# Unread products of the identity at PE's waits in a streaming encoder step

## The chip, the cores and the metric

The kernel runs on 1 core of one Trainium2 chip. TensorE (PE) multiplies, VectorE (DVE) and ScalarE (ACT) work element by element, GpSimd (POOL) helps, SyncE (SP) issues loads. Loading the weights of a product into PE's array is listed apart as PEld. The metric is the device time of one execution in microseconds, lower is better.

## What is computed

One inference step of two layers, for 512 prompt frames and 32 sample frames in one pass (T = 544 columns). Everything is f32. Cut to what matters here:

```python
def ffn_half(x, g_pre, g_post, w_gu, w_dn):
    return x + 0.5 * rmsnorm(swiglu(rmsnorm(x, g_pre), w_gu, w_dn), g_post)

def trunk_layer(l, x, ...):
    x = ffn_half(x, g[0], g[1], w_ffn_gu[l, 0], w_ffn_dn[l, 0])
    u = rmsnorm(x, g[2])
    qa, ka, va, qb, kb, vb = jnp.split(u @ w_in[l], 6, axis=-1)
    ...   # oa: band attention, 8 heads x 64; ob: differential attention, 4 heads x 128
    ob = rmsnorm(ob, subln_g[l]) * (1.0 - lam_init)
    mix = jnp.concatenate([oa, ob], axis=-1) @ w_out[l]
    x = x + rmsnorm(mix, g[3])
    oc = cross_attend(rmsnorm(x, g[4]) @ w_cq[l], mem_k, mem_v) @ w_co[l]
    x = x + rmsnorm(oc, g[5])
    return ffn_half(x, g[6], g[7], w_ffn_gu[l, 1], w_ffn_dn[l, 1])
```

Outputs are the two streams' results and the keys and values of every layer.

## The kernel before

Activations lie transposed: 8 blocks of 128 model columns on the partitions, 544 frames on the free axis, in two halves of 272 (half 0, half 1). A matrix product splits both sides into a high and a low part (`u_hi`, `u_lo`; `w_hi`, `w_lo`) and sums three products, `w_hi`·`u_hi`, `w_hi`·`u_lo`, `w_lo`·`u_hi`. This is `product` (line 607): three matmuls of 128x272 for each block and half. A **chunk** is all 8 blocks of one output tile, 24 matmuls for each half. SP loads the weights in chunks, ACT cuts `w_hi`, DVE takes the difference `w_lo`; both rings have two slots, and a slot is cut anew once PE has counted `chunk_done`.

Each engine runs its own list in the order in which it is written, and engines meet at semaphores. Nothing is planned while it runs.

**A hand-over** is the place where one stage ends and the next begins with a normalised input. The new `x` needs the norm of the last stage's output `y`: PE sums the squares over the partitions (`norm_y`, line 622), ACT takes the root, DVE the inverse, PE spreads it over the partitions (`spread_y`, lines 582 and 629: two turns and a small product of the identity), DVE multiplies `y` by it and adds it to `x`, ACT cuts `u_hi`, DVE `u_lo`. Half 0 is ahead of half 1. PE meanwhile runs `first_chunks`, in this order: first chunk of half 0, whose block k waits for `u_lo` of that block, with `norm_y` of half 1 before block 4 (`before`); `spread_y` of half 1 (`between`); second chunk of half 0; then both chunks of half 1, the first again block by block behind `u_lo`. `late_norms` calls it with `before` and `between` in five hand-overs: at the start of three feed-forward stages (all but the very first) and of the two combined input projections. The hand-over into cross-attention calls `first_chunks` without them. The pre-norm of the new stage is not applied to `u`; its sums of squares (`norm_x`) and its spread (`spread_x`) follow a little later, and the product's result is scaled by `r_pre`.

**Attention** follows a table of steps (`attention`, `OWN` for the two own head groups). Scores take two slots of PSUM in turn. At its end the outputs of the four differential heads, tiles 4 to 7, are turned (`"use": "out"`): the turn of tile 4 waits for `head_normed`, that is for the norm of all four heads, taken after the last value product; ACT takes the root, DVE scales `o_nat` head by head, and then DVE cuts `u_hi` and `u_lo` of every tile from the slot. `w_out` follows.

`ident` is an f32 identity of 128x128. The PSUM banks 0 and 1 take the two halves of the first chunk.

Of the kernel before, what the change touches and what calls it, by code (L numbers as in the profile page):

```python
# [72 lines left out]
def rows_of(i):  # L73
    return 128 if i < NT else SAMPLE
# [96 lines left out]
def build(nc, x_prompt, x_sample, mem_prompt, cache_a_k, cache_a_v, cache_b_k, cache_b_v,  # L171
# [8 lines left out]
    def place(name, shape, dtype=F32, offset=None):  # L180
        size = int(np.prod(shape[1:])) * 4
        if offset is None:
            offset = at[0]
            at[0] += (size + 31) // 32 * 32
        return nc.alloc_sbuf_tensor_at(name, shape, dtype, offset=offset)
# [17 lines left out]
    ident = place("ident", [128, 128])  # L203
# [82 lines left out]
    psum = nc.alloc_psum_tensor("psum", [128, 8, 512], F32)  # L286
# [61 lines left out]
    def slot_ap(slot, rows, n, start=0):  # L348
        return flat[0:rows, slot * 1024 + start:slot * 1024 + start + n]
# [32 lines left out]
    def settled(engine):  # L382


        engine.sem_inc(passed)
# [193 lines left out]
    def _(pe):  # L579
        def turn(out, src):  # L580
            rows = src.shape[0]
            return pe.transpose(out, src, ident[0:rows, 0:rows])  # L582
# [15 lines left out]
        def product(slot, b, bank, xs, start, stop, half=None):  # L598
            hi, lo = xs
            wh = w_hi[:, slot, b * 128:(b + 1) * 128]  # L600
            wl = w_lo[:, slot, b * 128:(b + 1) * 128]
            n = hi.shape[-1]
            halves = [(0, H), (H, T)] if n == T else [(0, n)]
            for w, xx, s0, s1 in ((wh, hi, start, False), (wh, lo, False, False), (wl, hi, False, stop)):
                for part, (c0, c1) in enumerate(halves):
                    if half in (None, part):
                        pe_last[0] = pe.matmul(psum[:, bank + part, 0:c1 - c0], w, xx[:, c0:c1], start=s0, stop=s1)  # L607

        def half_chunk(pair, slot, bank, inputs, blocks, half, first, last, before=None):

            pe.wait_ge(w_lo_ready, 2 * pair + slot + 1)
            for b, k in enumerate(blocks):
                if before:
                    before(k)
                product(slot, b, bank, inputs(k), first and b == 0, last and b == len(blocks) - 1, half)
            return pe_last[0]

        def token_sums(sums, half, bank, col):

            for i, start in enumerate(GROUPS):  # L620
                t = half * H + start
                mm = pe.matmul(psum[:, bank, col + i:col + i + 1], sums[:, t:t + 128], ones[:, 0:1], start=True, stop=True)  # L622
            return mm
# [31 lines left out]
        def first_chunks(pair, q, before=None, between=None):  # L655

            def arrived(half):
                def wait(k):
                    pe.wait_ge(u_lo_ready, 16 * q + 8 * half + k + 1)
                    if before and half == 0 and k == 4:  # L660
                        before()
                return wait
            half_chunk(pair, 0, 0, u_in, range(KD), 0, True, True, arrived(0))
            if between:
                between()
            half_chunk(pair, 1, 2, u_in, range(KD), 0, True, True)
            half_chunk(pair, 0, 0, u_in, range(KD), 1, True, True, arrived(1)).then_inc(chunk_done, 1)
            half_chunk(pair, 1, 2, u_in, range(KD), 1, True, True).then_inc(chunk_done, 1)

# [71 lines left out]
        def attention(l, steps):  # L741
            for step in steps:
                for it in step["uses"]:
                    slot = it["slot"] % 2
                    if it["slot"] >= 2:
                        pe.wait_ge(*slot_free(it["slot"] - 2, l))
                    if it["use"] == "cache":
                        tile, width = it["tile"], 128
                        if it["of_kind"] == "C":
                            pe.wait_ge(cmk_loaded, l * 16 + 16)  # L750
                            src = cmk_nat[:, tile, :]
                        else:
                            pe.wait_ge(kc_loaded[tile % 2], l * 64 + 32 * (it["of_kind"] == "B") + 16 * (tile // 2 + 1))
                            src = kc_nat[:, tile % 2, :]
                        for m in range(4):
                            mm = turn(slot_ap(slot, 128, 128, m * 128), src[:, m * 128:(m + 1) * 128])
                    elif it["use"] == "out":
                        if it["tile"] >= 4:
                            pe.wait_ge(head_normed, l * 8 + 2 * (it["tile"] - 3))
                        elif it["slot"] < OWN_COUNT["slot"]:  # L760
                            pe.wait_ge(o_kept, l * TOTAL["unit"] + 2 * (NT + 1) * (it["tile"] + 1))
                        else:
                            pe.wait_ge(o_kept, l * TOTAL["unit"] + OWN_COUNT["unit"] + (NT + 1) * (it["tile"] + 1))
                        for i in range(NT + 1):
                            mm = turn(slot_ap(slot, 128, rows_of(i), i * 128),
                                      o_nat[0:rows_of(i), it["tile"] % 4, i, :])
                    else:
                        mm = score(l, it, slot)
                    mm.then_inc(slot_ready, 1)
                for u in step["turn"]:  # L770
                    ub, rows = u["unit"] % 2, rows_of(u["i"])
                    if u["kind"] == "B":
                        pe.wait_ge(combined, l * TOTAL["combined"] + u["combined"] + 1)
                    else:
                        pe.wait_ge(expd, l * TOTAL["expd"] + u["scores"][0]["expd"] + 1)
                    if u["unit"] == 0:
                        pe.wait_ge(nat_kept, l * 32 + 32)
                    if u["unit"] >= 2:
                        pe.wait_ge(turned_kept, l * TOTAL["turned"] + UNITS[u["unit"] - 2]["turned"])
                    settled(pe)  # L780
                    p = probs_at(u["scores"][0])
                    n = keys_of(u)
                    for k in range((n + 127) // 128):
                        keys = min(128, n - k * 128)
                        mm = turn(psum[0:keys, 4 + ub, k * rows:(k + 1) * rows], p[0:rows, k * 128:k * 128 + keys])
                    mm.then_inc(turned, 1)
                for u in step["value"]:
                    ub, rows, h = u["unit"] % 2, rows_of(u["i"]), u["h"]
                    pe.wait_ge(turned_kept, l * TOTAL["turned"] + u["turned"])
                    if u["unit"] >= 2:  # L790
                        pe.wait_ge(o_kept, l * TOTAL["unit"] + u["unit"] - 1)
                    n = keys_of(u)
                    if u["i"] == NT:
                        if u["kind"] == "C":
                            pe.wait_ge(cmv_loaded, l * 16 + 16)
                        else:
                            pe.wait_ge(vc_loaded, l * 32 + (16 if u["kind"] == "A" else 32))

                    tiles = (n + 127) // 128
                    tile = h // 2 if u["kind"] == "A" else h  # L800
                    for k in range(tiles):
                        keys = min(128, n - k * 128)
                        at_ = tile * 128 + (512 if u["kind"] == "B" else 0)
                        if u["kind"] == "C":
                            v = (mv_nat if u["i"] < NT else cmv)[:, k, h * 128:(h + 1) * 128]
                        elif u["i"] == NT and k < 4:
                            v = vc[:, k, tile * 128:(tile + 1) * 128]
                        else:
                            v = v_nat[0:keys, k, at_:at_ + 128]
                        mm = pe.matmul(psum[0:rows, 6 + ub, 0:128],  # L810
                                       probs_t[0:keys, ub, k * rows:(k + 1) * rows], v,
                                       start=k == 0, stop=k == tiles - 1)
                    mm.then_inc(values_done, 1)
# [38 lines left out]
        for l in range(DEPTH):  # L852
# [65 lines left out]
            for m in range(KD + 1):  # L918
                if m < KD:
                    if m >= 2:  # L920
                        pe.wait_ge(kv_kept, l * 8 + m - 1)
                    chunk(base + AT_CKV + m // 2, m % 2, m % 2, lambda k: (m_hi[:, k, :], m_lo[:, k, :]), range(KD),
                          True, True, count=memory_norms if m == 0 else None).then_inc(chunk_done, 1)
# [802 lines left out]
```

## Time and profile before

| | us |
|---|---|
| median of 3 runs | 2788.9 |
| lowest, highest | 2785.92, 2790.43 |
| profiled execution, device time | 2787.24 |
| its span in the trace | 2785.4 |
| PE busy | 2610.1 (94%) |
| DVE busy | 1272.3 (46%) |
| ACT busy | 900.8 (32%) |
| mean granted clock of PE | 0.968 |

The span is the trace's own time, some 2 us less than the device time. Times in the trace count from the span's start; places are named by them. "[2.48 <-DVE w_lo L1285]" behind a row says that the engine sat idle for 2.48 us and which instruction released it. The end of a PE row is modelled, so distances between products are read from start to start. The granted clock is given as a share of 2.4 GHz: 1.00 is the full rate, 0.50 is 1.2 GHz, and a value between them is a stretch with both. "x2" behind a row means two records merged.

### The profile page before, as it was taken

The numbers are of one execution on the slowest core, as the hardware profiler recorded it, in microseconds if no ns is written. First come the engines' busy times: TensorE is split into PE (matmuls) and PEld (weight loads), VectorE is DVE, ScalarE is ACT, GpSimd is POOL, SyncE is SP. The second block draws the span as 40 slices with busy tenths as digits, with TensorE's granted clock in tenths as the row PEclk, the third lists the DMA queues.
The fourth block names the chain that finished last, engine by engine and source line by source line (L and its number), as shares of the span: only waits on it lengthen the run. The fifth ranks groups of instructions, "written<-read, shape, count | busy, mean of one in ns | idle before, by whom it ended". The sixth has DMA issues, their size and how long they took to land.

```text
span 2785.4 us, 48225 instructions
## 1 busy us (share of the span) xinstructions
PE 2610.1 (94%) x19513; PEld 2471.8 (89%) x19513; DVE 1272.3 (46%) x2307; ACT 900.8 (32%) x1576; POOL 67.9 (2%) x199
## 2 busy tenths in 40 slices
PE   7999998999898889999989999989898988999998
PEld 6999998986587789999989999989755977999998
DVE  4444325345846554442254442253457555444323
ACT  3222223224533432222232222232344534322221
POOL 1000000001100000000000000000111000000000
PEclk9999999999989999999999999999998998999999
DMA  5233332330023023233223233233310321223321
GB/s 178 85 88 90 91 91 86 116 120 25 24 91 105 18 68 90 84 95 94 67 69 88 85 92 93 73 101 116 105 40 31 92 75 31 83 83 90 97 84 64
DMA packets 383972, 229.81 MB, mean 83 GB/s; under 512 B 6636, under 2 KB 371198, under 8 KB 383840
## 3 DMA queue, kind: packets, MB, share of 16 engines
q1 hardware_dynamic: 378272, 206.59, 25.3%
q0 software_dynamic: 4368, 16.92, 1.7%
q10 hardware_dynamic: 1200, 4.46, 0.4%
q8 instruction: 93, 1.52, 0.2%
q14 instruction: 39, 0.32, 0.0%
HBM read 214.39 MB, written 18.79 MB: 84 GB/s over the span
## 4 chain that ended last, share of the span: by engine, by line
PE 83%; DVE 11%; ACT 2%; issue 2%; DMA 1%; DVEq 0%; SPq 0%; ACTq 0%
PE psum L607 73%; PE psum L810 3%; PE psum L582 3%; PE psum L829 2%; DVE u_lo L1280 2%; DVE w_lo L1285 2%; DVE x L1326 1%; DVE probs L1469 1%; PE psum L622 1%; DVE y_ffn L1320 1%; DVE y_mix L1320 1%; ACT w_hi L993 1%; PE psum L823 1%; PE psum L831 0%; DMA w_raw<-in_w_ffn_gu 0%
## 5 line engine op out<-in xcount | busy, mean ns | idle before, releaser
L607 PE MATMUL psum<-u_hi,w_hi 128*128 128x272 f32 x4096 | 906.8, 295 | 62.1 <-DVE w_lo L1285 24.2
L607 PE MATMUL psum<-u_hi,w_lo 128*128 128x272 f32 x4096 | 894.3, 292 | 0.0
L607 PE MATMUL psum<-u_lo,w_hi 128*128 128x272 f32 x4096 | 892.3, 292 | 0.0
L607 PEld LDWEIGHTS psum<-u_hi,w_hi 128*128 128x128 f32 x4096 | 671.7, 193 | 72.8 <-DVE u_lo L1280 28.3
L993 ACT ACTIVATE w_hi<-w_raw 128x1024 fp32r<-128x1024 f32 (+1 forms) x336 | 376.8, 1121 | 1105.6 <-PE psum L607 1091.2
L607 PEld LDWEIGHTS psum<-u_lo,w_hi 128*128 128x128 f32 x4096 | 672.5, 193 | 0.0
L607 PEld LDWEIGHTS psum<-u_hi,w_lo 128*128 128x128 f32 x4096 | 667.9, 193 | 0.0
L1285 DVE TENSOR_TENSOR w_lo<-w_raw,w_hi 128x1024 fp32r<-128x1024 f32 (+1 forms) x336 | 436.5, 1299 | 348.3 <-ACT w_hi L993 348.3
L607 PE MATMUL psum<-h_hi,w_hi 128*128 128x272 f32 x1408 | 305.7, 288 | 0.5
L607 PE MATMUL psum<-h_lo,w_hi 128*128 128x272 f32 x1408 | 304.5, 287 | 0.0
L607 PE MATMUL psum<-h_hi,w_lo 128*128 128x272 f32 x1408 | 304.4, 287 | 0.0
L607 PEld LDWEIGHTS psum<-h_hi,w_hi 128*128 128x128 f32 x1408 | 226.0, 189 | 1.3 <-DVE w_lo L1285 1.3
L607 PEld LDWEIGHTS psum<-h_lo,w_hi 128*128 128x128 f32 x1408 | 226.3, 188 | 0.0
L607 PEld LDWEIGHTS psum<-h_hi,w_lo 128*128 128x128 f32 x1408 | 226.2, 188 | 0.0
L1372 DVE TENSOR_TENSOR up<-psum,r_pre 128x544 f32<-128x544 f32 x88 | 63.7, 724 | 292.1 <-PE psum L607 292.1
L1368 DVE TENSOR_TENSOR gate<-psum,r_pre 128x544 f32<-128x544 f32 x88 | 63.8, 725 | 248.1 <-PE psum L607 232.7
L1013 ACT ACTIVATE square<-psum 128x544 f32<-128x544 f32 (+1 forms) x76 | 42.0, 552 | 333.8 <-PE psum L607 333.8
L1137 ACT ACTIVATE probs<-probs,negmax 128x256 f32<-128x256 f32 (+4 forms) x136 | 81.1, 596 | 140.8 <-DVE negmax L1469 140.6
L1297 DVE TENSOR_TENSOR sumsq<-sumsq,square 128x544 f32<-128x544 f32 (+1 forms) x60 | 36.7, 611 | 179.3 <-ACT square L1013 178.7
L1594 DVE TENSOR_TENSOR fresh<-psum,r_pre 128x544 f32<-128x544 f32 x48 | 34.6, 724 | 153.0 <-PE psum L607 146.6
L829 PE MATMUL psum<-qk,q_pad 128*128 128x384 f32 (+3 forms) x256 | 94.8, 471 | 3.2 <-DVE negmax L1469 2.2
L810 PE MATMUL psum<-v_nat,probs_t 128*128 128x128 f32 (+1 forms) x528 | 85.8, 290 | 10.2 <-ACT probs_t L993 8.9
(189 smaller groups left out, 2097.1 us busy)
## 6 DMA issues: line engine op xcount, KB each, us to landing
w_raw<-in_w_ffn_gu SPq DMA_DIRECT2D x176, 512.0 KB, 3.8
w_raw<-in_w_ffn_dn SPq DMA_DIRECT2D x64, 704.0 KB, 4.6
w_raw<-in_w_in SPq DMA_DIRECT2D x48, 512.0 KB, 3.7
w_raw<-in_w_out SPq DMA_DIRECT2D x16, 512.0 KB, 3.9
w_raw<-in_w_ckv SPq DMA_DIRECT2D x16, 512.0 KB, 3.8
bias_tab_dram<-bias_rev_dram POOLq DMA_DIRECT2D x1, 5120.0 KB, 21.3
table<-bias_tab_dram SPq DMA_DIRECT2D x16, 320.0 KB, 2.9
out<-k_nat POOLq DMA_DIRECT2D x4, 1024.0 KB, 5.0
```

The costliest lines, as they stand in the source:

```text
L582: return pe.transpose(out, src, ident[0:rows, 0:rows])
L607: pe_last[0] = pe.matmul(psum[:, bank + part, 0:c1 - c0], w, xx[:, c0:c1], start=s0, stop=s1)
L810: mm = pe.matmul(psum[0:rows, 6 + ub, 0:128], probs_t[0:keys, ub, k * rows:(k + 1) * rows], v, start=k == 0, stop=k == tiles - 1)
L829: return pe.matmul(slot_ap(slot, rows, keys_of(u)), q, k[:, 0:keys_of(u)], start=True, stop=True)
L993: return act.activation(out, src, ACT.Copy, scale=scale)
L1013: act.activation(sq, src, ACT.Square).then_inc(y_squared, 1)
L1137: act.activation(p, p, ACT.Exp, bias=negmax[0:rows, s % 8:s % 8 + 1], scale=-1.0, accum_out=rowsum[0:rows, s % 8:s % 8 + 1]).then_inc(expd, 1)
L1280: return dve.scalar_tensor_tensor(out=out, in0=a, scalar=scalar, in1=b, op0=op0, op1=op1)
L1285: dve.tensor_tensor(w_blocks(w_lo, slot, n), w_blocks(w_raw, slot, n), w_blocks(w_hi, slot, n).bitcast(F32), ALU.subtract).then_inc(w_lo_r ...
L1320: dve.tensor_tensor(part, part, r, ALU.mult).then_inc(y_normed, 1)
L1368: dve.tensor_tensor(two(gate[:, parity, :]), banks(4 * parity), two(r_pre[:, :]), ALU.mult).then_inc(gate_scaled, 1)
L1372: dve.tensor_tensor(two(up[:, parity, :]), banks(4 * parity + 2), two(r_pre[:, :]), ALU.mult).then_inc(up_scaled, 1)
```

## The change

`spin(n, out)` issues n products of the identity with itself, 128x128 in f32, each with start and stop set. Their result is overwritten by the next real product at the same place, and no instruction reads it. They are placed in three places:

- in `first_chunks`, if it was given `before`: 6 ahead of the first chunk of half 0, into bank 0
- also there: 20 between the second chunk of half 0 and the first of half 1, into bank 1
- in `attention`, 10 ahead of the wait for `head_normed` of tile 4, into the slot that this turn writes

That makes 5 x 26 products in the hand-overs and 2 x 10 in attention, 150 in all. No other engine's list changes, and PE's list is the old one with these rows put in.

```diff
--- before.py
+++ after.py
@@ -615,6 +615,11 @@
                 product(slot, b, bank, inputs(k), first and b == 0, last and b == len(blocks) - 1, half)
             return pe_last[0]
 
+        def spin(n, out):
+
+            for _ in range(n):
+                pe.matmul(out, ident[:, :], ident[:, :], start=True, stop=True)
+
         def token_sums(sums, half, bank, col):
 
             for i, start in enumerate(GROUPS):
@@ -660,10 +665,14 @@
                     if before and half == 0 and k == 4:
                         before()
                 return wait
+            if before:
+                spin(6, psum[:, 0, 0:128])
             half_chunk(pair, 0, 0, u_in, range(KD), 0, True, True, arrived(0))
             if between:
                 between()
             half_chunk(pair, 1, 2, u_in, range(KD), 0, True, True)
+            if before:
+                spin(20, psum[:, 1, 0:128])
             half_chunk(pair, 0, 0, u_in, range(KD), 1, True, True, arrived(1)).then_inc(chunk_done, 1)
             half_chunk(pair, 1, 2, u_in, range(KD), 1, True, True).then_inc(chunk_done, 1)
 
@@ -755,6 +764,8 @@
                         for m in range(4):
                             mm = turn(slot_ap(slot, 128, 128, m * 128), src[:, m * 128:(m + 1) * 128])
                     elif it["use"] == "out":
+                        if it["tile"] == 4:
+                            spin(10, slot_ap(slot, 128, 128))
                         if it["tile"] >= 4:
                             pe.wait_ge(head_normed, l * 8 + 2 * (it["tile"] - 3))
                         elif it["slot"] < OWN_COUNT["slot"]:
```

The places in PE's list, in the first hand-over between a feed-forward stage and the input projection. Before, where the first chunk of half 0 follows the down projection (`h_hi`, `h_lo` are its inputs):

```order
L607 MATMUL psum<-h_hi,w_hi 128x272
L607 MATMUL psum<-h_lo,w_hi 128x272
L607 MATMUL psum<-h_hi,w_lo 128x272
L607 MATMUL psum<-u_hi,w_hi 128x272 [waits u_lo_ready,w_lo_ready]
L607 MATMUL psum<-u_lo,w_hi 128x272
L607 MATMUL psum<-u_hi,w_lo 128x272
```

and the same place now:

```order
L607 MATMUL psum<-h_hi,w_hi 128x272
L607 MATMUL psum<-h_lo,w_hi 128x272
L607 MATMUL psum<-h_hi,w_lo 128x272
L621 MATMUL psum<-ident 128x128 x6
L607 MATMUL psum<-u_hi,w_hi 128x272 [waits u_lo_ready,w_lo_ready]
L607 MATMUL psum<-u_lo,w_hi 128x272
```

The six products stand ahead of the instruction that waits for `w_lo` and `u_lo`, and wait for nothing themselves. Between the halves, now:

```order
L607 MATMUL psum<-u_hi,w_hi 128x272
L607 MATMUL psum<-u_lo,w_hi 128x272
L607 MATMUL psum<-u_hi,w_lo 128x272
L621 MATMUL psum<-ident 128x128 x20
L607 MATMUL psum<-u_hi,w_hi 128x272 [waits u_lo_ready,w_lo_ready]
L607 MATMUL psum<-u_lo,w_hi 128x272
L607 MATMUL psum<-u_hi,w_lo 128x272
```

The twenty follow the last product of the second chunk of half 0, and the first block of half 1 is queued behind them. At the end of attention, where tile 4 is turned, before:

```order
L810 MATMUL psum<-vc,probs_t 32x128 x3
L810 MATMUL psum<-v_nat,probs_t 32x128
L582 MATMUL psum<-ident,o_nat 128x128 [waits head_normed,biased]
L582 MATMUL psum<-ident,o_nat 128x128 x3
L582 MATMUL psum<-ident,o_nat 128x32
```

and now:

```order
L821 MATMUL psum<-vc,probs_t 32x128 x3
L821 MATMUL psum<-v_nat,probs_t 32x128
L621 MATMUL psum<-ident 128x128 [waits biased]
L621 MATMUL psum<-ident 128x128 x9
L582 MATMUL psum<-ident,o_nat 128x128 [waits head_normed]
```

The wait for the slot (`biased`) moved to the first of the ten; the wait for the norm stays with the turn.

## Rows read from the trace of the kernel before

**Rows 1.** The page's chain that ended last, by engine: shares of the span

```profile
PE 83%; DVE 11%; ACT 2%; issue 2%; DMA 1%; DVEq 0%; SPq 0%; ACTq 0%
```

**Rows 2.** PE's waits, whole span: waiting line, releaser, us in total, times, longest

```profile
PE psum L607 <- DVE u_lo L1280: 24.1, 21, 2.1
```

**Rows 3.** Timeline, PE, 439 to 463: start, us, operation, count, [idle before, releaser]

```profile
439.09 0.39 PE L607 MATMUL psum<-u_hi,w_hi 128*128 128x272 f32 x1 [2.48 <-DVE w_lo L1285]
...
442.58 1.44 PE L622 MATMUL psum<-ones,sumsq 128*128 128x1 f32 x6 [0.67 <-DVE u_lo L1280]
...
446.99 0.60 PE L607 MATMUL psum<-u_hi,w_hi 128*128 128x272 f32 x1 [1.40 <-DVE u_lo L1280]
...
449.23 0.57 PE L607 MATMUL psum<-u_hi,w_hi 128*128 128x272 f32 x1
449.60 0.43 PE L607 MATMUL psum<-u_lo,w_hi 128*128 128x272 f32 x1
449.83 0.43 PE L607 MATMUL psum<-u_hi,w_lo 128*128 128x272 f32 x1
...
458.55 0.40 PE L607 MATMUL psum<-u_hi,w_hi 128*128 128x272 f32 x1 [1.15 <-DVE u_lo L1280]
...
462.54 0.52 PE L607 MATMUL psum<-u_hi,w_hi 128*128 128x272 f32 x2
```

**Rows 4.** Chain in order of time: a dense stretch, start, us, records

```profile
490.91 6.02 PE psum L607 x48
```

**Rows 5.** Windows, PE: window, length, busy (records), granted clock, DMA share, GB/s

```profile
440.00:452.00 12.00, 9.92 (x43) 0.50 0.50 143
452.00:454.00 2.00, 2.00 (x14) 0.73 1.00 378
984.00:986.00 2.00, 2.00 (x12) 0.61 0.42 128
1817.00:1819.00 2.00, 1.18 (x9) 0.86 0.00 0
1833.00:1835.00 2.00, 2.00 (x10) 0.50 0.00 0
```

**Rows 6.** Timeline, PE, hand-over at 973: second chunk, first product after half 1

```profile
984.16 0.57 PE L607 MATMUL psum<-u_hi,w_hi 128*128 128x272 f32 x1
...
997.47 0.52 PE L607 MATMUL psum<-u_hi,w_hi 128*128 128x272 f32 x2
```

**Rows 7.** Value products in attention: two groups of the timeline, the page's group

```profile
636.63 1.16 PE L810 MATMUL psum<-v_nat,probs_t 128*128 128x128 f32 x8
...
638.48 1.06 PE L810 MATMUL psum<-vc,probs_t 128*32 128x128 f32 x8
...
L810 PE MATMUL psum<-v_nat,probs_t 128*128 128x128 f32 (+1 forms) x528 | 85.8, 290 | 10.2 <-ACT probs_t L993 8.9
```

**Rows 8.** Timeline at the turn of the heads' outputs: DVE, then PE

```profile
770.22 0.77 DVE L1438 TENSOR_SCALAR u_hi<-psum,sub_gain 128x544 fp32r<-128x544 f32 x1
...
768.04 2.61 PE L582 MATMUL psum<-ident,o_nat 128*128 128x128 f32 x10 [2.60 <-DVE o_nat L1611]
...
776.42 0.82 PE L607 MATMUL psum<-u_hi,w_hi 128*128 128x272 f32 x2 [1.70 <-DVE u_lo L1280]
```

**Rows 9.** Timeline, PE, hand-over at 1813

```profile
1813.00 0.39 PE L607 MATMUL psum<-u_hi,w_hi 128*128 128x272 f32 x1 [2.48 <-DVE w_lo L1285]
...
1816.49 0.83 PE L622 MATMUL psum<-ones,sumsq 128*128 128x1 f32 x6 [1.39 <-DVE u_lo L1280]
...
1820.29 0.59 PE L607 MATMUL psum<-u_hi,w_hi 128*128 128x272 f32 x1 [2.11 <-DVE u_lo L1280]
...
1822.52 0.57 PE L607 MATMUL psum<-u_hi,w_hi 128*128 128x272 f32 x1
...
1831.85 0.42 PE L607 MATMUL psum<-u_hi,w_hi 128*128 128x272 f32 x1 [1.16 <-DVE u_lo L1280]
...
1837.24 0.42 PE L607 MATMUL psum<-u_hi,w_hi 128*128 128x272 f32 x2
```


## The prediction

> **What bounds the kernel now.** I read the chain of waits first, then PE's waits, then PE's own rows with the granted clock beside them. The chain ends on PE for 83% of the span and on DVE for 11% [rows 1]. The change adds only work for PE, so it can save time in one way alone, by keeping PE's clock up, and only where PE is last. PE's waits show where: 24.1 us for `u_lo` in 21 waits, beside those for `w_lo` and for the heads' `o_nat` [rows 2, 3, 8]. A large part of them lies in the five hand-overs that carry the new products (at about 439, 973, 1394, 1813 and 2346 us) and before the two attention outputs (768 and 2140 us).
>
> One hand-over, at 439 us [rows 3]. PE waits 2.48 us for `w_lo`, runs four blocks of half 0, waits until 442.58 for block 4 and the sums, and until 446.99 for blocks 6 and 7. Then come the spread of `inv_y`, from 449.23 the second chunk of half 0 (24 products), and the two chunks of half 1 (48 products), paced by `u_lo` until 458.55. At 462.54 PE goes on with full products. Products stand 0.227 us apart here (449.60 to 449.83) against 0.125 us in dense stretches (48 in 6.02 us) [rows 3, 4]. The granted clock says why: 0.50 from 440 to 452, the lower level of 1.2 GHz, back at 2.4 GHz within 452 to 454 [rows 5].
>
> The cold clock costs less than it seems. It delays the end only where PE is the last to arrive: in the sums, in blocks 6 and 7 and in the spread, because DVE waits for the spread. After that DVE paces half 1, and the cold second chunk fits into waits. From the first product of the second chunk to the first after half 1 PE takes 13.31 us at 449 (462.54 - 449.23), with 17 cold products, and the same 13.31 us at 984 (997.47 - 984.16), with some 6 cold ones [rows 3, 6]: the clock's return, late or early, made no difference.
>
> **What one filler costs.** A product of two f32 operands is two records of PE: the three sums stand as x6. The nearest rows are the value products of attention: two groups of 8 records last 1.16 and 1.06 us, and one record 0.29 us on the mean, which leaves 7 steps of 0.124 and 0.110 us [rows 7]. For a run of 12 to 40 alike I take 0.115. Bounds: 0.105 below, since a product of 272 columns needs 0.125 and these have 128 columns in a wider type, 0.125 above. So 6 products are 1.4 us, 20 are 4.6 us (4.2 to 5.0), 10 are 2.3 us. At the low clock f32 records stand some 0.24 us apart (10 in 2.61 us) [rows 8], which would make it 2.9, 9.7 and 4.8 us.
>
> On a page: the Trainium skill ("TensorE: Matmul & The Clock Gate", section "Back-to-back issue gap") gives about 81 ns for each matmul of 128 columns in a stream with weight loads. By it the 20 products would be an estimated 3.2 us and my total would fall by 7 us, to about -2. The trace's f32 rows read 0.110 to 0.124, so the sum goes by them.
>
> **Part 1, six products before half 0.** 1.4 us in a wait of 2.48 us: nothing to pay, PE is back 1 us before `w_lo`. If that cover were gone it would be 1.4 us each. They should keep the clock up until the first blocks. What that is worth one hand-over of before already shows, the one at 1813, where the clock stayed up through the blocks and sums and fell only within 1817 to 1819 [rows 5]. There blocks 6 and 7 started 3.80 us after the sums (1816.49 to 1820.29) instead of 4.41 us (442.58 to 446.99) [rows 3, 9]. So 0.6 us in each of the other four. But in the same hand-over the clock then fell in the two waits around the sums (1.39 and 2.11 us idle), and the blocks at 1820.29, the spread and the start of the second chunk ran cold. The six fillers put nothing into those waits. So I expect each changed hand-over to look like 1813 up to the spread, and that one to stay as it is.
>
> **Part 2, twenty products between half 0 and half 1.** They stand after the second chunk of half 0. PE's work from that chunk's first product to the end of half 1 becomes 72 products at 0.125 us = 9.0, restarts 0.2, fillers 4.6: 13.8 us at the full clock, against 13.31 us now, where DVE sets the pace. So the fillers do not fit: they exceed the waits that are there, even warm. To that comes what of the second chunk is cold, 0.10 us a product: 0.6 us (6 products) to 1.7 us (17), and 0.3 us more where it starts 0.6 us earlier, on average 1.2 us. Before, this was hidden; now PE is the last. 15.0 us, so +1.7 us, less 0.6 us from part 1: +1.1 us, in four hand-overs +4.4 us. At 1813 the stretch takes 14.72 us now (1822.52 to 1837.24), since the clock fell a second time while PE waited for `u_lo`: 0.50 in 1833 to 1835 [rows 5, 9]. The fillers remove that fall; 15.0 - 14.72 = +0.3 us, and another 0.3 us since ACT cuts the next weights and squares x only when the first chunk of half 1 is done. Who waits behind: ACT's `w_hi`, the squares and DVE's `sumx` (for which PE waits near 465), then the next chunks; nothing after half 1 in a feed-forward hand-over has slack, as PE runs densely to the spread of `inv_x`. So delays go to the end one to one.
>
> **Part 3, ten products before the turn of tile 4.** 2.3 us in a wait of 2.60 us [rows 8]: hidden at the full clock. The ten turns after it would be warm, but DVE does not wait for them: it runs without idle time before `u_hi` at 770.22, and PE starts the output projection on `u_lo` at 776.42. Between lie ten more turns and waits, the last of 1.70 us, so the projection should start cold as now. I take 0. Bounds: +2 us each if the ten ran cold (4.8 us in 2.6), -1.9 us each if the clock held through to the projection (18 products 0.10 us faster).
>
> **Sum.** 4.4 + 0.6 + 0 = +5.0 us. Made against the profiled execution, 2787.24 us, that is 2792.2; the median of before is 1.7 us above that execution, and I put the same difference on it: 2788.9 + 5.0 = 2793.9 us.
>
> **The rivals.**
> A, the clock is held (faster). If the fillers keep 2.4 GHz through the waits at the sums too, the spread comes some 1.5 us earlier (0.6 sums, 0.6 blocks 6 and 7, 0.3 spread), against +0.5 us for 13.8 in place of 13.31: -1.0 us in four, and at 1813 -0.9 - 0.9 = -1.8. Sum -6, time about 2783; with a warm output projection -10. For it: the fillers give PE work just ahead, and the clock did stay up over a wait of 2.48 us before 1813 [rows 9]. Against it: 1813 itself. It decides by the clock at blocks 6 and 7. The Trainium skill (same page, section "HAM oscillation — how this bites in real kernels") blames the fall on waits between bursts that are longer than those that remain here, and recommends dense work; by that rule the clock would hold and this rival's time would come. The trace speaks against it: the clock fell at 1818 with idle times of 1.39 and 2.11 us.
> B, the clock returns late (slower). If the sums stay cold and the clock comes back as late as at 439 in every hand-over, the surcharge is 1.7 to 2.0 us and nothing is won first: 15.7 - 13.3 = +2.4 in four and +1 at 1813, sum +11, time about 2800. For it: the row at 440 to 452. Against it: at 984 it was back within 984 to 986 [rows 5]. It decides where over 10 products of the second chunk run cold.
> C, it comes out even, between -3 and +2 us: fillers at 0.105 us or below (-2 us), the clock back at once in most places (-4 us), or the fillers without any effect on the clock and mostly in waits. Time about 2788.
>
> **How the numbers follow.** Forecast 0.57, A 0.16, B 0.12, C 0.15. A measurement of this kernel tells some 0.2% (5.6 us) from no change. The forecast's own range is +2 to +8 us, so 0.23 of its 0.57 lie beyond +5.6. Slower: 0.23 + B 0.12 = 0.35. Faster: most of A, 0.14. Same: 0.34 + 0.02 + 0.15 = 0.51. The range leaves out the outer part of A and of B: 2784 to 2801.
>
> **What would show it.** Right: f32 records of `ident` 0.11 to 0.125 us apart; clock 1.0 at the first blocks and sums, 0.50 at blocks 6 and 7; no wait for `u_lo` left in half 1; the stretch from the second chunk's start to the first product after half 1 at 14.4 to 15.6 us against 13.31; half-1 products dense and warm; 776.42 unchanged against its own attention. Wrong: clock 1.0 at the spread (A), waits for `u_lo` still there after the twenty (cheaper fillers), or a late turn of tile 4.

## The result, and the profile after

The change makes the kernel slightly slower: the median of 20 runs is 2792.9 us against 2788.3 us for 20 runs of the kernel before. The ratio is 1.0018, 95% interval 1.0011 to 1.0026, that is +4.6 us where +5.0 us had been forecast (the interval is +3 to +7 us). One point of caution first: the profiled execution of after took 2786.4 us, the lowest of its 20 runs, with a span of 2784.6 us, 0.8 us less than before's. So the profile does not show the loss as a whole; it shows what the hand-overs cost, and something else that went better in this one execution.

The page's chain, after (before: [rows 1], PE 83% and DVE 11%):

```profile
PE 85%; DVE 10%; ACT 2%; issue 2%; DMA 1%; DVEq 0%; SPq 0%; ACTq 0%
```

PE's wait for `u_lo` in the waits of after (us in all, number, longest; before 24.1 us in 21 waits [rows 2]):

```profile
PE psum L607 <- DVE u_lo L1291: 12.8, 8, 2.2
```

The waits halved, PE took a larger share of the chain, and the time did not fall: a wait was filled, and a little more than filled. The first hand-over shows where. The timeline of PE of after (start, us, operation; before [rows 3]):

```profile
435.94 1.50 PE L621 MATMUL psum<-ident 128*128 128x128 f32 x12
438.57 0.40 PE L607 MATMUL psum<-u_hi,w_hi 128*128 128x272 f32 x1 [1.13 <-DVE w_lo L1296]
...
442.06 0.83 PE L627 MATMUL psum<-ones,sumsq 128*128 128x1 f32 x6 [1.38 <-DVE u_lo L1291]
...
445.86 0.59 PE L607 MATMUL psum<-u_hi,w_hi 128*128 128x272 f32 x1 [1.49 <-DVE u_lo L1291]
...
448.09 0.57 PE L607 MATMUL psum<-u_hi,w_hi 128*128 128x272 f32 x1
...
451.90 4.62 PE L621 MATMUL psum<-ident 128*128 128x128 f32 x40
...
462.37 0.41 PE L607 MATMUL psum<-u_hi,w_hi 128*128 128x272 f32 x2
```

The same hand-over's granted clock (window, length, PE busy, clock, DMA share, GB/s), and in the last line that of the second hand-over, whose first block starts at 971 here and at 973 in before:

```profile
438.00:442.00 4.00, 2.08 (x12) 1.00 0.47 131
443.00:449.00 6.00, 4.51 (x20) 0.50 0.39 119
451.00:456.00 5.00, 5.00 (x46) 1.00 0.80 297
456.00:462.00 6.00, 6.00 (x51) 1.00 0.00 1
976.00:985.00 9.00, 7.60 (x34) 0.50 0.20 58
```

Read from top to bottom: the six fillers end 1.1 us before `w_lo` is there; the clock is at 2.4 GHz over the first blocks (before it was at 1.2 GHz from 440 on [rows 5]); it falls at the sums, between a wait of 1.38 us and one of 1.49 us, so the blocks behind the sums, among them 6 and 7, the spread and the start of the second chunk run at 1.2 GHz (products 0.227 us apart); the twenty take 4.6 us at the full clock; and after them PE has no wait left up to the first full product. That stretch, from the second chunk's first product to the first after half 1, is 14.28 us (462.37 - 448.09), where before had 13.31 us.

Read in the same way, the five hand-overs of both profiles (us, from start to start). The last column goes on to the sums of `x` (`ones,sumx`), the next thing for which PE may have to wait:

| hand-over at | sums to blocks 6, 7: before, after | second chunk to end of half 1: before, after | first block to end: before, after | first block to sums of `x`: before, after |
|---|---|---|---|---|
| 439 | 4.41, 3.80 | 13.31, 14.28 | 23.45, 23.80 | 26.47, 26.92 |
| 973 | 4.41, 4.27 | 13.31, 15.33 | 23.99, 25.86 | 30.12, 31.86 |
| 1394 | 4.41, 3.86 | 13.30, 14.21 | 23.43, 23.79 | 29.55, 29.79 |
| 1813 | 3.80, 3.94 | 14.72, 14.09 | 24.24, 23.76 | 26.49, 26.88 |
| 2346 | 4.41, 4.33 | 13.31, 15.28 | 23.99, 25.87 | 30.12, 31.87 |
| sum | | | 119.10, 123.08 | 142.75, 147.32 |

Up to the end of half 1 the hand-overs cost 4.0 us more. At 1813 this mark comes too early, as PE's timeline shows, first in before (the hand-overs at 439 and at 1813):

```profile
465.56 1.50 PE L622 MATMUL psum<-ones,sumx 128*128 128x1 f32 x12 [0.51 <-DVE sumx L1344]
...
1839.49 1.39 PE L622 MATMUL psum<-ones,sumx 128*128 128x1 f32 x12
```

and in after:

```profile
465.49 1.60 PE L627 MATMUL psum<-ones,sumx 128*128 128x1 f32 x12 [0.71 <-DVE sumx L1355]
...
1837.86 1.50 PE L627 MATMUL psum<-ones,sumx 128*128 128x1 f32 x12 [0.71 <-DVE sumx L1355]
```

At 1813 before reached the end of half 1 late and then had no wait for `sumx`; after reached it earlier and waited 0.71 us. So the 0.5 us that after seems to win there is a loss of 0.4 us one step later. Up to the sums of `x` the five hand-overs cost 4.6 us more. How much of that is the change and how much this pair of executions is less sure: the kernel with the ten alone and the one with the held projection, both described below, have the hand-overs of before, and took 144.8 and 144.9 us to the same mark.

The rest of the profiled execution was 5.4 us shorter than before's (2784.6 - 147.32 against 2785.4 - 142.75). No work was changed there but the ten products in attention. The clock was low for less of it: in windows of 2 us, PE was busy at 1.2 GHz outside the hand-overs for an estimated 100 us in before and 90 us in after. One such place, in attention, as PE's window in before:

```profile
699.00:705.00 6.00, 5.71 (x22) 0.50 0.00 0
```

and the same window in after:

```profile
699.00:705.00 6.00, 5.09 (x36) 1.00 0.11 40
```

The places where the clock falls are not the same ones in each execution. The 20 runs of before spread over 10 us and those of after over 14 us, and in after the mean granted clock goes with the time: 0.974 in the shortest run, 0.970 in the longest.

The last place, at the turn of the heads' outputs, PE's timeline in after (before: [rows 8]):

```profile
766.14 4.58 PE L621 MATMUL psum<-ident 128*128 128x128 f32 x20
770.55 1.54 PE L582 MATMUL psum<-ident,o_nat 128*128 128x128 f32 x10
...
777.56 0.82 PE L607 MATMUL psum<-u_hi,w_hi 128*128 128x272 f32 x2 [2.19 <-DVE u_lo L1291]
```

and DVE's there:

```profile
771.37 0.79 DVE L1449 TENSOR_SCALAR u_hi<-psum,sub_gain 128x544 fp32r<-128x544 f32 x1 [0.32 <-PE psum L582]
```

In this execution attention ended at the low clock, and the ten took 4.58 us where the prediction had 2.3. They ended after the turn could have begun, and DVE, which had not waited before, waited 0.32 us.

### The profile page after: what moved, and what is told of

Same layout as the page of the kernel before. It is cut to its first block, busy times and chain, and to the rows that moved or that the text cites. A ratio compares the mean times of both kernels' runs of the same rounds, so it can differ in the third digit from the quotient of the medians.

```text
span 2784.6 us, 48823 instructions
## 1 busy us (share of the span) xinstructions
PE 2630.0 (94%) x19813; PEld 2495.4 (90%) x19813; DVE 1272.6 (46%) x2307; ACT 898.9 (32%) x1576; POOL 67.6 (2%) x199
## 4 chain that ended last, share of the span: by engine, by line
PE 85%; DVE 10%; ACT 2%; issue 2%; DMA 1%; DVEq 0%; SPq 0%; ACTq 0%
PE psum L607 73%; PE psum L821 3%; PE psum L582 3%; PE psum L840 2%; DVE w_lo L1296 2%; PE psum L621 1%; DVE u_lo L1291 1%; DVE probs L1480 1%; DVE x L1337 1%; PE psum L627 1%; ACT w_hi L1004 1%; PE psum L834 1%; DVE y_mix L1331 1%; PE psum L842 0%; DVE y_ffn L1331 0%
```

## The experiments

Each difference is against the kernel of the change; each ratio against the kernel before, from interleaved runs. A line `pass` stands where products are left out. None leaves out or changes any part of the computation: the products in question are read by nobody. The kernel with forty, the first one with filled waits and the two with all of it together have only 5 or 6 runs each, the others 11 or 12.

**The six alone.**

```diff
-                spin(20, psum[:, 1, 0:128])
+                pass
-                            spin(10, slot_ap(slot, 128, 128))
+                            pass
```

> Only the six products ahead of half 0 are left of the change. My theory (they fit into the wait for w_lo, and keep the clock at 2.4 GHz over the first blocks and the sums): blocks 6 and 7 of half 0 start 3.8 us after the sums instead of 4.4 us, in four of five hand-overs, of which some is lost again where the clock comes back later: -1 to -2 us against before. If the six themselves were the loss (they delay the first block), +1.4 us in each of five hand-overs, +7 us. If they have no effect on the clock, 0.

Measured: 2785.7 against 2788.0 us, ratio 0.9991 (0.9980 to 1.0003), so -2.4 us with an interval that just includes no change. The sums to blocks 6 and 7 took 3.88, 4.33, 3.80, 3.80 and 3.80 us. The time from the first block to the end of half 1 was 118.4 us over the five, 0.7 us less than before's 119.1; in two of them the clock fell again in the waits of half 1, as it had at 1813 before (14.67 and 14.49 us for the stretch). Up to the sums of `x` it was 142.0 us against 142.75. The six are not the loss; that they gain anything lies within the noise of the medians.

**The twenty alone.**

```diff
-                spin(6, psum[:, 0, 0:128])
+                pass
-                            spin(10, slot_ap(slot, 128, 128))
+                            pass
```

> Only the twenty products between half 0 and half 1 are left. My theory (they exceed the waits of half 1 by 0.5 us with a warm second chunk, and every cold product of that chunk is now paid for): more than the whole change, since the sums stay cold: +6 to +8 us against before, and no wait for u_lo left in half 1. If the loss of the change lies in the six or in attention, 0 or less here; if the twenty hold the clock and that pays, below 0.

Measured: 2792.1 against 2788.0 us, ratio 1.0022 (1.0012 to 1.0031). By the ratio that is +6 us, the lower end of what was expected; by the two medians it is +4.0 us, below it. No wait for `u_lo` in half 1; first block to end summed 124.2 us, +5.1 us, and to the sums of `x` 148.4 us, +5.7 us. The loss sits here. That the six give back a part of it is what the profiles show (148.4 us here, 147.3 us in the change); the times of the two kernels (1.0022 and 1.0018) are too close to tell.

**The ten in attention alone.**

```diff
-                spin(6, psum[:, 0, 0:128])
+                pass
-                spin(20, psum[:, 1, 0:128])
+                pass
```

> Only the ten products ahead of the turn of tile 4 are left. My theory (hidden in the wait for head_normed, and DVE paces what follows): 0, between -1 and +1 us; the output projection starts cold as before. If they hold the clock through to the projection: -3.8 us. If they run at the low clock or past the wait: +2 to +4 us.

Measured: 2787.8 against 2788.0 us, ratio 1.0001 (0.9992 to 1.0010): nothing. In both layers of this profile they ran at the full clock, 2.50 us, and the time from the last value product to the projection was 11.38 us, that of before to the last digit. In the profiles where the last value products ran at the low clock it was 11.6 us without the ten (the kernel with the twenty alone, both layers) and 11.9 to 12.0 us with them, as in the change. In the kernel with forty, where the clock came back during the ten (3.03 us), it was 11.6 us. So they are free or cost 0.3 to 0.4 us, by the clock that they find. In this profile one hand-over, which has no products of the change, had a second fall of the clock: 15.56 us from the second chunk to the end of half 1 at 1394, 13.3 us in the other four.

**Forty in place of twenty.**

```diff
-                spin(20, psum[:, 1, 0:128])
+                spin(40, psum[:, 1, 0:128])
```

> The whole change, with 40 products in place of 20 between the halves. My theory says that PE is the last to arrive already with 20, so that all of the added time is paid: 20 products of 0.23 us (two records of 0.115 us) in five hand-overs, +23 us against the change, +28 us against before (1.010). If waits were left behind the twenty, less: with 1 us of wait left in each hand-over +23 us against before, with 2 us +18 us.

Measured: 2815.6 us, ratio 1.0094 (1.0079 to 1.0108). By the ratios that is +26 us against before and +21 us against the change (1.0018), by the medians +28 and +23 us. PE's timeline in its first hand-over:

```profile
449.37 0.57 PE L607 MATMUL psum<-u_hi,w_hi 128*128 128x272 f32 x1
...
453.14 9.09 PE L621 MATMUL psum<-ident 128*128 128x128 f32 x80
...
468.09 0.41 PE L607 MATMUL psum<-u_hi,w_hi 128*128 128x272 f32 x2
```

The stretch is 18.72 us, 4.44 us more than the change's 14.28, and the fillers are 4.47 us longer. Everything that is added between the halves is paid at once: with the twenty PE was already the last.

**Ten in place of twenty.**

```diff
-                spin(20, psum[:, 1, 0:128])
+                spin(10, psum[:, 1, 0:128])
```

> The whole change with 10 products in place of 20 between the halves (2.3 us instead of 4.6). My theory: PE's work over second chunk and half 1 is then 11.5 us warm and about 12.7 with some cold products, below DVE's pace of 13.31, so waits for u_lo come back in half 1, the fillers cost nothing, the gain of the six (some 0.5 us each) stays and no second fall of the clock is left: -2 to -5 us against before (0.9985), that is -7 to -9 us against the change. If the twenty cost time for another reason than their length (a start of the stream, memory traffic), only half of the loss goes: +2 us against before.

Measured: 2784.3 against 2786.9 us, ratio 0.9991 (0.9983 to 1.0000), -2.6 us. PE's timeline in its fourth hand-over:

```profile
1819.92 0.57 PE L607 MATMUL psum<-u_hi,w_hi 128*128 128x272 f32 x1
...
1824.09 2.39 PE L621 MATMUL psum<-ident 128*128 128x128 f32 x20
...
1829.24 0.39 PE L607 MATMUL psum<-u_hi,w_hi 128*128 128x272 f32 x1 [0.49 <-DVE u_lo L1291]
...
1833.23 0.52 PE L607 MATMUL psum<-u_hi,w_hi 128*128 128x272 f32 x2
```

The stretch is 13.31 us, in all five between 13.29 and 13.32, although blocks 6 and 7 and the start of the second chunk still ran cold: DVE's pace is back as the bound, and there was no second fall. First block to end sums to 116.5 us, -2.6 us against before, and to the sums of `x` 141.0 us, -1.8 us; that the first is just the medians' difference is chance. Half the fillers turn the loss into a gain about as large as its own uncertainty.

**Filling the waits in which the clock fell** (rival A of the prediction, made true by more products).

```diff
+                    if before and half == 0 and k in (4, 6):
+                        spin(6 if k == 4 else 7, psum[:, 1, 0:128])
-                spin(20, psum[:, 1, 0:128])
+                spin(10, psum[:, 1, 0:128])
```

> As the kernel with 10 between the halves, and with 6 products more behind block 3 of half 0 (ahead of the sums) and 7 more behind block 5, in the two waits in which the clock fell in the change. It tests the rival that the clock can be held through a hand-over. If so, sums, blocks 6 and 7, the spread and the second chunk all run at 2.4 GHz, the spread comes 1.5 us earlier than before and DVE's pace follows: -1.5 us in four hand-overs, more where before had a second fall, -7 to -9 us against before (0.997). If the clock falls in spite of it, the fillers run at 0.24 us a record and delay the sums: +5 us or more.

Measured: 2777.4 us, ratio 0.9963 (0.9951 to 0.9976), -9.5 us. Its first hand-over, PE's timeline:

```profile
441.75 1.50 PE L621 MATMUL psum<-ident 128*128 128x128 f32 x12
...
444.83 1.72 PE L621 MATMUL psum<-ident 128*128 128x128 f32 x14
...
447.10 0.39 PE L607 MATMUL psum<-u_hi,w_hi 128*128 128x272 f32 x1 [0.55 <-DVE u_lo L1293]
...
448.36 0.37 PE L607 MATMUL psum<-u_hi,w_hi 128*128 128x272 f32 x1
...
461.66 0.52 PE L607 MATMUL psum<-u_hi,w_hi 128*128 128x272 f32 x2
```

and the window of PE over all of it (busy, clock, DMA share, GB/s):

```profile
438.00:462.00 24.00, 20.97 (x161) 1.00 0.42 138
```

The clock stays at 2.4 GHz. From blocks 6 and 7 to the second chunk it takes 1.26 us (447.10 to 448.36) where before took 2.24 us [rows 3], and the sums cost 0.6 us less: the spread comes 1.6 us earlier, and DVE's pace of 13.3 us starts from there. First block to end sums to 110.3 us, -8.8 us, and to the sums of `x` 134.75 us, -8.0 us.

**The same with twenty again, and with none between the halves.** The first keeps `spin(20, ...)`, the second has

```diff
-                spin(20, psum[:, 1, 0:128])
+                pass
```

beside the two added lines of the filled kernel.

> The filled hand-overs with 20 products between the halves again instead of 10: the price of the twenty where no product is cold. Prediction's term: 72 products at 0.125, restarts 0.2 and fillers 4.6 are 13.8 us against DVE's pace of 13.31, so +0.5 us a hand-over, +2.5 us against the kernel with ten (0.9963): about 0.9972 of before, -8 us. If the twenty cost their full difference of 2.3 us a hand-over in spite of the waits, +11.5 us, 1.0004 of before; if PE were not the last, 0.9963 as with ten.

> The filled hand-overs without any product between the halves. If the ten there do nothing once the clock is held over the sums, 0.9963 as with them. My theory: without them PE idles three times while it waits for u_lo in half 1 (0.3 to 0.6, 1.1 and 1.2 us or more, since it arrives earlier than before), the clock falls there in some hand-overs and the end of half 1 runs cold: +2 to +6 us against the kernel with ten, 0.9970 to 0.9985 of before.

With twenty: 2776.7 against 2787.0 us, ratio 0.9965 (0.9953 to 0.9976). That is not to be told from ten (0.9963), so the medians neither show nor exclude the expected 2.5 us; they exclude 11.5. The profile has the number itself, on PE's timeline:

```profile
445.38 0.37 PE L607 MATMUL psum<-u_hi,w_hi 128*128 128x272 f32 x1
...
448.48 4.63 PE L621 MATMUL psum<-ident 128*128 128x128 f32 x40
...
458.95 0.42 PE L607 MATMUL psum<-u_hi,w_hi 128*128 128x272 f32 x2
```

13.57 us, the same within 0.01 in all five hand-overs, against 13.3 with ten: 0.3 us too long where no product is cold, 1.3 us in all. In the change the excess over 13.31 us was 6.6 us in the five hand-overs. So about four fifths of it is cold products, and the fillers' length only takes away the room for them.

With none: 2779.1 us, ratio 0.9971 (0.9960 to 0.9981), about 2 us more than with ten, at the low end of what was expected; the two intervals overlap. In its profile the stretch took 14.70, 13.29, 15.16, 15.16 and 14.46 us: in four of five the clock fell in the waits of half 1, and in one it did not. Its clock there:

```profile
1406.00:1412.00 6.00, 5.82 (x30) 0.61 0.02 5
```

So fillers between the halves are worth having in these profiles (13.3 us in all five hand-overs with ten); the medians alone do not prove it.

**Holding the clock up to the output projection.** No filler in the hand-overs; the ten ahead of tile 4 stay.

```diff
+                    if it["use"] == "out" and it["tile"] >= 6:
+                        spin(8 if it["tile"] == 6 else 3, psum[:, 6, 0:128])
...
+            spin(8, psum[:, 6, 0:128])
             pe.wait_ge(split_lo, l * TOTAL["split"] + OWN_COUNT["split"])
```

> Only at the end of attention: ten products ahead of the turn of tile 4, 8 ahead of tile 6, 3 ahead of tile 7, 8 ahead of the output projection, all in waits for DVE; no filler in the hand-overs. If the clock is held through to the projection, its first 18 products run at 0.125 us instead of 0.227: -1.9 us in each of two layers, -3.8 us against before (0.9986). If my reading of the waits is off and the fillers delay the turns that DVE waits for, +1 to +4 us. If the clock falls anyway, 0.

Measured: 2782.5 against 2786.9 us, ratio 0.9985 (0.9976 to 0.9994), -4.4 us. The clock, where before had 1.2 GHz until 780:

```profile
770.00:782.00 12.00, 12.00 (x96) 1.00 0.18 66
```

This was the other end of part 3's bounds, and the ten ahead of the first turn alone could not do it (the experiment with the ten alone). Its profile accounts for only half of the 4.4 us. The fillers make the projection start later after the last value product (12.33 and 12.19 us in the two layers, before 11.38), and the first turn of the memory behind the projection comes 1.0 and 1.15 us sooner (42.49 and 42.35 us after the last value product, before 43.50).

**All of it together, and two more places.** The filled hand-overs and the held projection in one kernel; then also 12 products ahead of the last turn of the memory values and 8 ahead of the first chunk of cross-attention's queries:

```diff
+                    if m == KD:
+                        spin(12, psum[:, 5, 384:512])
                     pe.wait_ge(kv_kept, l * 8 + t + 1)
...
+            spin(8, psum[:, 5, 384:512])
             pe.wait_ge(kv_nat, l * 8 + 8)
```

> The fillers of the filled hand-overs and those up to the output projection together. The parts lie in different places and each shifts all that follows, so they should add: -8 - 3.8, about -12 us against before (0.9957). If the gain of one is given back at the other's place, less than the larger of the two.

> All held, and in addition 12 products ahead of the last turn of the memory values (PE waits 3.27 us there) and 8 ahead of the first chunk of the cross-attention's queries (2.19 us), where the clock fell in the trace of the kernel with all held, with some 20 products at 0.227 us after it. If it is held, -2 us in each of two layers: about 0.9937 - 0.0014 = 0.9923 of before. If the twelve (2.8 us) run into the low clock, or past the wait, +1 to +3 us.

Measured: 2770.2 against 2786.9 us, ratio 0.9937 (0.9922 to 0.9952), then 2765.1 against 2787.0 us, ratio 0.9923 (0.9909 to 0.9937). The parts add at least: -9.5 and -4.4 make -13.9 us against -16.7 measured, within the intervals; the -12 us (0.9957) that had been expected was too little and lies outside the interval. The two further places bring the expected 0.14%, 4 us, though the intervals of the two kernels overlap. The clock in the second, over the end of the memory's projection, the hand-over to the queries and their chunks:

```profile
848.00:884.00 36.00, 33.70 (x275) 1.00 0.43 132
```

This version is faster than the kernel before by 22 us and than the change by some 27 us.

## Why the prediction was right, step by step

The mechanism is shown: the loss needs the twenty, it goes with half of them, and it grows with forty by the full time that they add. That the number came within 0.4 us is in part luck, since one execution of a kernel and the next differ by more, and since single terms missed in both directions.

- **PE at the hand-overs, DVE's pace behind it.** Right. DVE's 13.3 us from the second chunk to the end of half 1 stood in every kernel in which PE's own work fitted and the clock did not fall again: with none, with six and with ten fillers.
- **The price of a filler.** 0.115 us a record was taken, the trace has 4.62 us for 40 records and 1.50 us for 12, so 0.111 us for each one more (3.12 over 28). At the low clock 20 records took 4.41 us up to the next row (766.14 to 770.55), 0.22 us each where 0.24 had been taken. The Trainium skill ("TensorE: Matmul & The Clock Gate", section "Back-to-back issue gap") has about 81 ns for each matmul at 128 columns; these f32 records do not agree with it.
- **Part 1.** Right in kind: covered by the wait, blocks and sums at the full clock. The gain was mis-sized, 0.6 us expected in each of four hand-overs and 0.6, 0.1, 0.6 and 0.1 us seen: in two of them the clock fell before or in the sums, which come 4.03 us after the first block there and 3.49 us in the others, in before as in after. I had read the hand-over at 1813 as the rule and it was the better half.
- **Part 2.** Right: no wait left, and the cold products are what is paid. 13.8 us was 13.57 us; the cold products came to 0.7, 1.8, 0.6, 0.5 and 1.7 us, 1.1 on average where 1.2 was taken; so 14.6 us where 15.0 had been expected. The smaller stretch and the smaller gain of part 1 cancelled: in the four hand-overs the loss up to the end of half 1 was 4.5 us, where 4.4 had been summed, but as 0.4, 1.9, 0.4 and 1.9 us and not as 1.1 in each.
- **The second fall at 1813.** Gone, as expected: 14.09 us for 14.72, where the sum had 15.0. What it was worth shows only at the sums of `x`: 26.88 us for 26.49, so +0.4 us where +0.6 had been summed. The fall had cost before less than the 1.4 us that the stretch showed, because PE otherwise waits 0.5 us for `sumx`. It is also no mark of this one hand-over: in the two other profiles with the hand-overs of before it came at 1394, and in one of them at 439 too.
- **Part 3.** 0 was taken. With the ten alone it is 0; in the profile of the change attention ended cold, and it cost 0.3 to 0.4 us in each layer, against attention that ends cold without the ten. My bound of +2 us was too wide: DVE was busy scaling heads until shortly before the turn was done.
- **Rival A.** It was not what the change did (0.50 at blocks 6 and 7 in all five), but its working was sound: with the waits filled it came at -9.5 us, where -7 to -9 had been expected from it with ten in place of twenty. The Trainium skill's advice of dense work (same page, section "HAM oscillation — how this bites in real kernels") agrees with that trace. The reading that the prediction gave as the rival's, that waits as short as these leave the clock up, does not agree with the change: the clock fell with waits of 1.38 and 1.49 us.
- **Rival B.** It did not come in the medians, but two of five hand-overs looked like it: 15.33 and 15.28 us.

What stays open: why one hand-over keeps the clock over the same waits in one execution and not in the next. The runs show that it happens, not what decides it. Open is also how much of the change's +4.6 us is the hand-overs alone, for the reason given under the table.

## What to carry to other kernels

Here filler work at one wait did not keep PE's clock up in the later ones, so follow the clock from wait to wait up to the work that counts; a wait left open can give the gain away. The waits at the sums, left open, gave away most of it (the change with ten between the halves -2.6 us, with them filled -9.5 us), those of half 1 about 2 us. Size a filler below the wait that remains when everything around it runs at the full clock, not by the wait that a cold trace shows: ten cost nothing between the halves here, and the products from twenty to forty were paid in full. And ask first who is last at each place: a cold stretch of PE under the pace of another engine costs nothing until the filler makes PE the last.

## What the hardware showed that I had not expected

- A filler reads the clock that it finds: the same 20 records took 2.50 us in one profile and 4.58 us in another, so a filler that fits at 2.4 GHz can overrun its wait at 1.2 GHz. In a third profile the clock came back while they ran, and they took 3.03 us.
- Products whose result is overwritten unread, in f32 and of an identity that is nearly all zeros, can fill a wait as far as the clock is concerned: with 40 such records among the 275 of PE, the granted clock was 1.00 over 36 us on end. No run here shows how few would do.
- The same kernel's runs spread by 10 to 14 us, more than the change is worth; with 20 runs of each the interval is still +3 to +7 us, and the one profiled execution of after was faster than the profiled one of before.
- What a stretch gains or loses has to be followed to the next place where PE can wait: 0.5 us won up to the end of half 1 at 1813 was 0.4 us lost at the sums of `x`, some 3 us later.
